# Where the first weight product begins: the two halves of y turned at other places, and the second weight chunk rounded by VectorE

## The reference

```python
    bu_re = jnp.einsum('blgh,gph->lbgp', u, bb_re)
    bu_im = jnp.einsum('blgh,gph->lbgp', u, bb_im)
    ...
    _, _, s_re, s_im = lax.associative_scan(
        _ssm_combine, (a_seq_re, a_seq_im, bu_re, bu_im), axis=0)
    y = (jnp.einsum('lbgp,ghp->blgh', s_re, c_re.astype(f32))
         - jnp.einsum('lbgp,ghp->blgh', s_im, c_im.astype(f32)))
    y = y.reshape(bsz, seq, D_MODEL) + d_skip.astype(f32) * x.astype(f32)
    h = jax.nn.gelu(y).astype(x.dtype)
    val, gate = jnp.split(h @ w_glu, 2, axis=-1)
    z = val * jax.nn.sigmoid(gate)
    return (z @ w_out).astype(x.dtype)
```

## Time and profile before

| | before |
|---|---|
| median of 3 runs | 1367.01 us (1366.93 to 1367.15) |
| the profiled execution | 1366.22 us |
| its span in the profile | 1364.4 us |
| PE busy | 1337.6 us, 98% |
| VectorE busy | 934.9 us, 69% |
| ACT busy | 674.0 us, 49% |
| GpSimd busy | 58.8 us, 4% |
| share of PE in the chain that ended last | 88% |

### The profile page before, as it was taken

One profiled execution on the slowest core, in us unless ns is written; L12 is line 12 of the kernel. 1 busy time (PEld: TensorE's weight loads), 2 busy tenths in 40 slices (PEclk: granted clock), 3 DMA queues, 4 the chain that ended last, 5 costly groups with the idle time before them and its releaser, 6 DMA issues.

```text
span 1364.4 us, 27289 instructions
## 1 busy us (share of the span) xinstructions
PE 1337.6 (98%) x11455; PEld 1300.5 (95%) x11455; DVE 934.9 (69%) x1253; ACT 674.0 (49%) x833; POOL 58.8 (4%) x31
## 2 busy tenths in 40 slices
PE   6899999999999999999999999999999999999998
PEld 4599999999999999999989999999999999999998
DVE  8966976547865976656896687764457867877542
ACT  5774643334765643334656544444344644544331
POOL 6910000000000000000000000000000000000000
PEclk9999999999999999999999999999999999999999
DMA  8676576665443586666454546566664435556761
GB/s 154 156 186 184 135 208 184 185 186 183 147 134 108 140 216 184 184 186 182 128 155 126 184 155 197 182 181 185 182 186 126 152 124 186 193 187 180 193 182 52
DMA packets 342542, 227.90 MB, mean 167 GB/s; under 512 B 22600, under 2 KB 337264, under 8 KB 342320
## 3 DMA queue, kind: packets, MB, share of 16 engines
q1 hardware_dynamic: 340928, 226.33, 57.5%
q10 hardware_dynamic: 1520, 0.20, 0.1%
HBM read 224.40 MB, written 1.05 MB: 165 GB/s over the span
## 4 chain that ended last, share of the span: by engine, by line
PE 88%; DVE 6%; ACT 3%; issue 1%; POOL 1%; DMA 0%; SPq 0%; ACTq 0%; DVEq 0%; POOLq 0%
PE PS L414 27%; PE PS L415 27%; PE PS L416 27%; DVE w_lo L395 2%; ACT w_hi L390 1%; PE PS L1312 1%; DVE xn L1101 1%; DVE xn L1106 1%; PE PS L1714 0%; PE PS L2378 0%; PE PS L1296 0%; DVE sqr L1066 0%; PE PS L1324 0%; PE PS L2389 0%; DVE raw_lo L1059 0%
## 5 line engine op out<-in xcount | busy, mean ns | idle before, releaser
L395 DVE TENSOR_TENSOR w_lo<-raw,w_hi 128x2048 fp32r<-128x2048 f32 x207 | 473.4, 2290 | 157.4 <-ACT w_hi L390 156.9
L414 PE MATMUL PS<-x_hi,w_hi 128*128 128x256 f32 x1792 | 511.7, 286 | 0.5 <-DVE w_lo L395 0.4
L415 PE MATMUL PS<-x_lo,w_hi 128*128 128x256 f32 x1792 | 506.9, 283 | 0.0
L416 PE MATMUL PS<-x_hi,w_lo 128*128 128x256 f32 x1792 | 506.8, 283 | 0.0
L390 ACT ACTIVATE w_hi<-raw 128x2048 fp32r<-128x2048 f32 x207 | 395.1, 1909 | 214.2 <-PE PS L416 212.6
L414 PE MATMUL PS<-hid_hi,w_hi 128*128 128x256 f32 x1248 | 354.2, 284 | 0.0
L415 PE MATMUL PS<-hid_lo,w_hi 128*128 128x256 f32 x1248 | 353.2, 283 | 0.0
L416 PE MATMUL PS<-hid_hi,w_lo 128*128 128x256 f32 x1248 | 353.2, 283 | 0.0
L414 PEld LDWEIGHTS PS<-x_hi,w_hi 128*128 128x128 f32 x1792 | 343.3, 192 | 5.2 <-issue 2.6
L415 PEld LDWEIGHTS PS<-x_lo,w_hi 128*128 128x128 f32 x1792 | 343.4, 192 | 0.1
L416 PEld LDWEIGHTS PS<-x_hi,w_lo 128*128 128x128 f32 x1792 | 343.4, 192 | 0.0
(11 more groups left out here) (387 smaller groups left out, 1324.4 us busy)
## 6 DMA issues: line engine op xcount, KB each, us to landing
raw<-in_w_ff_dram SPq DMA_DIRECT2D x128, 512.0 KB, 4.6
raw<-in_ffn_w_gu_dram SPq DMA_DIRECT2D x88, 512.0 KB, 5.1
raw<-in_w_in_dram SPq DMA_DIRECT2D x68, 512.0 KB, 4.7
raw<-in_sb_w_qkv_dram SPq DMA_DIRECT2D x24, 512.0 KB, 4.6
raw<-in_ffn_w_down_dram SPq DMA_DIRECT2D x20, 512.0 KB, 4.7
raw<-in_ssm_w_glu_dram SPq DMA_DIRECT2D x16, 512.0 KB, 5.7
raw<-in_w_out_dram SPq DMA_DIRECT2D x16, 512.0 KB, 4.5
raw<-in_ssm_w_out_dram SPq DMA_DIRECT2D x8, 512.0 KB, 4.5
```

The source lines that it names most:

```text
L395: nc.vector.tensor_tensor(w_lo[s][:, :], raw[s][:, :], w_hi[s][:, :].bitcast(F32), ALU.subtract).then_inc(lo_done, 1)
L414: nc.tensor.matmul(dst, lhs_hi, r_hi, start=start, stop=False, skip_group_check=True)
L415: nc.tensor.matmul(dst, lhs_hi, r_lo, start=False, stop=False, skip_group_check=True)
L416: return nc.tensor.matmul(dst, lhs_lo, r_hi, start=False, stop=stop, skip_group_check=True)
```

## The change

Three things change around the first weight product:

- The turning of a half becomes a function, `mixed_turned(pe, half)`. Half 0 is turned between the carried products of slot 2 and of slot 3.
- Half 1 is turned inside `glu_first`, behind the first four matmuls.
- ACT no longer rounds chunk 1. VectorE does, in one copy of 128x2048 between its last part of `state` and its first copy of y.

```diff
@@ glu_first
                         nc.tensor.matmul(dst, hi[:, kt, m, :], x_hi[:, kt, :], start=kt + m == 0, stop=False, skip_group_check=True)
                         nc.tensor.matmul(dst, lo[:, kt, m, :], x_hi[:, kt, :], start=False, stop=False, skip_group_check=True)
+                    if kt == 0:
+                        mixed_turned(pe, 1)
                     pe.wait_ge(xl_done, kt + 1)
@@ s5_tensor
                 if slot == 0 and ends:
                     pe.wait_ge(st_act, 14)
+                if slot == 3:
+                    mixed_turned(pe, 0)
                 for i in ones:
...
+        def mixed_turned(pe, half):
             pe.wait_ge(xt_done, 4)
-            for half in range(2):
-                pe.wait_ge(y_act, half + 1)
-                pe.wait_ge(y_dve, half + 1)
-                for t in range(SL):
-                    for blk in range(4):
-                        rows = slice(SC * blk, SC * blk + SC)
-                        last = nc.tensor.transpose(PS[:, 4 * half + blk, SC * t:SC * t + SC],
-                                                   y_half[rows, half, t, :], ident[rows, rows])
-                last.then_inc(yt_ready, 1)
+            pe.wait_ge(y_act, half + 1)
+            pe.wait_ge(y_dve, half + 1)
+            for t in range(SL):
+                for blk in range(4):
+                    rows = slice(SC * blk, SC * blk + SC)
+                    last = nc.tensor.transpose(PS[:, 4 * half + blk, SC * t:SC * t + SC],
+                                               y_half[rows, half, t, :], ident[rows, rows])
+            last.then_inc(yt_ready, 1)
@@ s5_scalar
             residual(2)
-            act.wait_ge(raw_ready[1], 32)
             outputs(0)
             residual(3)
-            nc.scalar.activation(w_hi[1][:, 0:CH // 2], raw[1][:, 0:CH // 2], ACT.Copy)
             outputs(1)
-            nc.scalar.activation(w_hi[1][:, CH // 2:CH], raw[1][:, CH // 2:CH], ACT.Copy).then_inc(hi_done, 1)
@@ s5_vector
                 V.tensor_tensor(dst, src, zero, ALU.add).then_inc(st_dve, 1)
+            dve.wait_ge(raw_ready[1], 32)
+            V.tensor_copy(w_hi[1][:, :], raw[1][:, :]).then_inc(hi_done, 1)
             for half in range(2):
                 dve.wait_ge(y_ready, 2 * half + 2)
                 V.tensor_copy(*y_places(2 * half + 1)).then_inc(y_dve, 1)
```

## The result

| | before | after |
|---|---|---|
| median of 11 runs | 1367.01 us (1365.62 to 1367.79) | 1368.83 us (1365.69 to 1372.46) |
| ratio | | 1.002, 95% interval 1.0013 to 1.0028 |
| profiled execution, its span | 1366.22, 1364.4 us | 1365.94, 1364.2 us |

What follows compares the result with a forecast made beforehand. PE, busy 98% of the span, bounds the kernel. VectorE's copy, held by GpSimd to 73.36, delays the first x_lo matmul from 75.97 to 77.42: 1367.01 + 1.45 = 1368.5 us, range 1366.6 to 1369.6.

Steps and rivals of the forecast that it cites:

- What bounds the kernel: From the first weight product on, PE (98% busy) is one solid matmul stream; a shift of its start carries through one for one.
- the mark: PE's first matmul with x_lo in the first weight product: 75.97 us before the change, forecast at 77.42.
- The hold: VectorE's copy of w_hi[1] is blocked until 0.14 us before GpSimd's w_lo[0] ends, ending at 73.36; chance as summed 0.80.
- The sum of 1.45 us: From the blocked copy's end through both halves and slot 3, the first x_lo matmul moves from 75.97 to 77.42.
- the second rival: PE's clock falls to 1.2 GHz for the rest of the first chunk's product: 1373.7 us; chance 0.04 including other losses.
- all other great losses: Any other loss over 2.7 us, sharing a chance of 0.04 with the fall of PE's clock.
- The price of 5.3 us: Time added if PE ran at 1.2 GHz for the rest of the first chunk's product, giving 1373.7 us.
- GpSimd is first by 0.9 us: GpSimd's w_lo[0] starts at 67.70, ahead of VectorE's copy at 68.60; the change touches neither start.
- the sum's 1368.5: Forecast time of the changed kernel: the timed median before, 1367.01 us, plus 1.45 us.
- the rival "not held": VectorE's copy isn't blocked by GpSimd and ends at 69.83; first x_lo matmul at 75.67, time 1366.7 us; chance 0.13.
- the first rival's 0.3 us: Gain if VectorE's copy isn't blocked by GpSimd: 0.30 us faster, 1366.7 us; chance 0.13.

Runs made afterwards that it cites:

- held trace: Trace of the unaltered changed kernel, profiled again, in which VectorE's rounding copy lasted 4.70 us beside GpSimd's w_lo[0]; that kernel timed again: 1369.19 us.
- wait filled: Changed kernel plus two matmuls of 512 and 256 columns, results overwritten, in PE's wait ahead of turning half 0: 1367.80 us, ratio 1.0013 to the kernel before.
- plain wait: Changed kernel plus a semaphore wait for GpSimd's w_lo[0] ahead of VectorE's rounding copy: 1370.7 us over six runs, ratio 1.0031 to the kernel before.
- rounding alone: Kernel before with chunk 1 rounded by VectorE's copy, PE's order left as before: 1368.43 us, ratio 1.0008.
- split instruction: Changed kernel with GpSimd's w_lo[0] made by two instructions of 1024 columns instead of one of 2048: 1366.0 us, ratio 1.0001 to the kernel before.
- one-port copy: Changed kernel with VectorE's rounding of chunk 1 done by adding a zero from PSUM, one SBUF input: 1365.95 us, ratio 0.9996 to the kernel before.
- copy moved: Changed kernel with VectorE's copy of chunk 1 behind its first copy of y instead of ahead of it: 1366.19 us, ratio 0.9999 to the kernel before.
- order turned round: Changed kernel with GpSimd's w_lo[0] also waiting until VectorE's copy of chunk 1 is done: 1366.87 us, ratio 1.0002 to the kernel before.

## Why the prediction was right and wrong

**What bounds the kernel**: right, with two exceptions. The shift of the mark was carried to the end: in the held trace the mark is 2.3 us later (2.5 from the scan's end) and the span 2.5 us longer, and with the wait filled 1.4 and 1.6. Where the clock was still low behind the mark more was lost (plain wait: mark 4.3 us later, span 6.1). And in the trace with the rounding alone the mark is only 0.1 us later but the span 1.1, of which 0.69 is an issue gap of PE at 79.57.

**The hold**: right, where GpSimd is first. The copy's end, GpSimd's end less 0.14 plus 1.23, was met to 0.01 us in six traces (73.14, 74.69, 73.08, 73.41, 72.92, and 72.14 with the split instruction).

**The sum of 1.45 us**: right for the case it describes. The wait-filled kernel has the mark at 77.38 against 77.42.

**The step that failed** is the second rival: "The granted clock is 1.00 (2.4 GHz) from 60 to 76 us, and that stretch has a wait of 1.55 us, so one of 1.75 is hardly new". I gave it and all other great losses 0.04 together. In the timed executions 10 of 23 had a mean clock of 0.996 or less, against 9 of 101 before, and they took 1369.5 us and more. The clock's part in the held trace is about 1.1 us (2.5 less 1.45), by PE's slot 3 (1.86 for 1.08) and what followed. The price of 5.3 us was too high for that trace, where the clock was at 0.50 for about 3.4 us (0.58 on average from 74 to 78) and PE's wait ahead of half 1 went with it. It was less far off for the longest executions: 1372.5 is 4.0 us above the sum's 1368.5. What the row for the clock could say was that in one execution nothing fell; I read it as a property of the kernel. The executions of the kernel before show how rare such a one is: 10 of 101 have a mean clock of 1.000, as the profiled one has. Which wait loses the clock in an execution stays open.

**A step that failed the other way**: "GpSimd is first by 0.9 us (67.70 against 68.60), and neither start is touched by the change". The starts are touched by the clock ahead of the change, from one execution to the next. In the profiled one VectorE was first, and the rival "not held" came out at its own mark, 75.61 against 75.67.

**The forecast as a whole**: 1368.5 us against 1368.83, but by luck: that median lies among three kinds of execution (two of which I had as rivals), the quicker ones with the copy first and the slower ones with the clock lost on either side of the one I summed. The measured loss is 1.8 to 2.5 us and not 1.45, and on the edge of 0.2% instead of well within it.

**What of the change was worth something**: little either way. With the hold out of the way (one-port copy, copy moved, order turned round, instruction split) all four kernels lie within 0.05% of the one before, as the first rival's 0.3 us (0.02%) said: by its sum, turning half 0 earlier makes slot 3 later by its 0.6 us. The best, the one-port copy, is at 0.9996 (0.9987 to 1.0005) and can't be told from no change.

## What to carry to other kernels

Before a one-input copy in SBUF is given to VectorE, look at what GpSimd runs at that moment, and at what is queued behind the copy: a hold costs nothing in itself, and all of its length for whoever waits for the next instruction. A wait of PE ahead of a dense stream can have two prices, its length and the clock that may be lost behind it, and the second shows only in some executions: take the clock of all runs into the estimate, not that of one trace. Where two engines' starts lie within a microsecond, fix their order by a semaphore or work out both orders.

## What the runs showed that I had not expected

The granted clock fell to 0.50 behind a wait of only 1.11 us (with 0.53 us of PE work in the 2 us around it), and in another kernel stayed there for most of 11 us, although PE was busy for 9.8 of them. The kernel before loses some clock in most executions as well, at little cost: its runs with a mean of 0.997 have a median of 1366.8 us, those with 0.999 of 1365.6, but those with 1.000 of 1366.0. Where it is lost there isn't shown, as the only trace is one without a loss; seven of the traces of the changed and edited kernels have a fall between 60 and 70 us. And a held VectorE instruction takes its turn between two GpSimd instructions that follow each other at once.
